# Sums of weight blocks for a seven-product block scheme: from accumulating transfers to VectorE additions in the raw buffers

## What is computed

```python
def swiglu(h, w_in, w_out):
    gate, up = jnp.split(h @ w_in, 2, axis=-1)
    return (jax.nn.silu(gate) * up) @ w_out
```

## Time and profile before

| | |
|---|---|
| median of three runs | 1367.05 us (1366.12 to 1367.58) |
| the profiled execution, its own time | 1369.06 us |
| its span | 1367.1 us |
| mean granted TensorE clock | 0.988 |
| TensorE / VectorE / ScalarE / GpSimd busy | 95% / 63% / 43% / 11% |

### The profile page before, as it was taken

One profiled execution on the slowest core, in us unless ns is written; L12 is line 12 of the kernel. 1 busy time (PEld: TensorE's weight loads), 2 busy tenths in 40 slices (PEclk: granted clock), 3 DMA queues, 4 the chain that ended last, 5 costly groups with the idle time before them and its releaser, 6 DMA issues. The chain is left out here.

```text
span 1367.1 us, 18309 instructions
## 1 busy us (share of the span) xinstructions
PE 1305.5 (95%) x6963; PEld 1072.3 (78%) x6963; DVE 867.1 (63%) x1512; ACT 588.4 (43%) x1113; POOL 147.5 (11%) x160
## 2 busy tenths in 40 slices
PE   3799999999999999999999999999999999999998
PEld 3678788889788888888888876655887888888886
DVE  4889787647567755666565759876463574457235
ACT  3256674545453222321224655687353342333231
POOL 1002020004400000000000001221011001000000
PEclk9899999999999999999999999999999999999999
DMA  9654522110516555555543120010139468736221
GB/s 322 196 172 149 185 66 90 63 62 2 185 43 208 199 188 175 197 201 185 189 138 93 44 74 31 32 32 32 62 101 232 129 153 229 173 90 183 65 92 62
DMA packets 110408, 175.17 MB, mean 128 GB/s; under 512 B 9709, under 2 KB 74490, under 8 KB 110330
## 3 DMA queue, kind: packets, MB, share of 16 engines
q1 hardware_dynamic: 90970, 113.30, 25.2%
q0 software_dynamic: 19360, 60.82, 15.8%
HBM read 172.01 MB, written 2.10 MB: 127 GB/s over the span
## 5 line engine op out<-in xcount | busy, mean ns | idle before, releaser
L411 PE MATMUL ps<-h_hi,w_hi 128*128 128x512 f32 x872 | 343.7, 394 | 1.8 <-DVE w_lo L395 1.4
L413 PE MATMUL ps<-h_hi,w_lo 128*128 128x512 f32 x872 | 340.2, 390 | 0.0
L412 PE MATMUL ps<-h_lo,w_hi 128*128 128x512 f32 x872 | 339.9, 390 | 0.0
L395 DVE TENSOR_TENSOR w_lo<-raw,w_hi 128x1024 fp32r<-128x1024 f32 x156 | 189.5, 1224 | 183.8 <-ACT w_hi L389 183.1
L389 ACT ACTIVATE w_hi<-raw 128x1024 fp32r<-128x1024 f32 x158 | 165.3, 1051 | 97.8 <-PE ps L2444 69.7
L411 PEld LDWEIGHTS ps<-h_hi,w_hi 128*128 128x128 f32 x872 | 164.2, 188 | 35.8 <-ACT silu_g L2266 1.3
L413 PEld LDWEIGHTS ps<-h_hi,w_lo 128*128 128x128 f32 x872 | 164.0, 188 | 35.0
L412 PEld LDWEIGHTS ps<-h_lo,w_hi 128*128 128x128 f32 x872 | 164.3, 188 | 33.0
L514 DVE SCALAR_TENSOR_TENSOR ada_acc<-ada_in,c_act,ada_acc 128x512 f32<-128x512 f32 x154 | 115.6, 751 | 4.2
L2266 ACT ACTIVATE silu_g<-ps 128x512 f32<-128x512 f32 x44 | 26.2, 595 | 127.6 <-PE ps L413 118.2
L1070 DVE SCALAR_TENSOR_TENSOR tmp<-conv_u,conv_t,tmp 128x512 f32<-128x512 f32 x72 | 54.2, 752 | 37.0 <-ACT tmp L1064 34.9
(11 more groups left out here) (429 smaller groups left out, 2485.7 us busy)
## 6 DMA issues: line engine op xcount, KB each, us to landing
raw<-in_ffn_w_in_dram SPq DMA_DIRECT2D x44, 1024.0 KB, 5.4
ada_in<-in_ada_w_dram POOLq DMA_DIRECT2D x40, 1024.0 KB, 5.7
raw<-in_gdn_w_in_dram SPq DMA_DIRECT2D x16, 1024.0 KB, 5.8
ada_in<-in_ffn_w_out_dram POOLq DMA_DIRECT2D x14, 1024.0 KB, 10.9
raw<-in_ffn_w_out_dram SPq DMA_DIRECT2D x12, 1024.0 KB, 5.1
ada_in<-in_ada_w_dram SPq DMA_DIRECT2D x4, 1024.0 KB, 9.4
x_t<-in_x_dram SPq DMA_DIRECT2D x2, 2048.0 KB, 9.9
early_slab<-in_ada_w_dram SPq DMA_DIRECT2D x4, 1024.0 KB, 14.1
```

Source lines behind the costliest of these rows:

```text
L395: ops.tensor_tensor(lo, raw_tile(s, kc) if src is None else src, f32(hi), ALU.subtract).then_inc(lo_done, 1)
L411: nc.tensor.matmul(out_, hi[:, k, :], r_hi[:, k, :], start=k == 0, stop=False)
L412: nc.tensor.matmul(out_, hi[:, k, :], r_lo[:, k, :], start=False, stop=False)
L413: last = nc.tensor.matmul(out_, lo[:, k, :], r_hi[:, k, :], start=False, stop=k == kc - 1)
```

## The change

The accumulating transfers go. GpSimd's queue now loads W10 and W11 as they are into `W_SUM[0]` and `W_SUM[1]`; SP loads W00 and W01 into the raw buffers. VectorE makes the sums in place: `raw[0]` becomes W00+W01, then +W11, then +W10, each when the split of the content before is done, and `raw[1]` becomes W01+W11. The products come in the order in which these sums arise: W00, W00+W01, W00+W01+W11, W11, W01+W11, W10, the sum of all. Two products now follow each other in one bank pair, so 14 evacuations are left of 16. The next part's first load into `raw[0]` waits for the last sum's split (`all_lo`), that into `raw[1]` for the split of W01+W11; SP issues them in this order.

```diff
-                    early = (4 * q - 4, 4 * q - 2) if layer in SEVEN and p and isinstance(i, int) and i == 0 else None
+                    early = seven_free(layer, p - 1) if layer in SEVEN and p and isinstance(i, int) and i == 0 else None
...
-                    sp.dma_start(as_quarter(raw[side])[:, k0:k1, :], quarter(layer, p, side, side)[:, k0:k1, :])\
+                    sp.dma_start(as_quarter(raw[side])[:, k0:k1, :], quarter(layer, p, 0, side)[:, k0:k1, :])\
                         .then_inc(raw_in[side], 16)
-            sp.wait_ge(lo_done, u + 6)
-            sp.dma_start(W_SUM[layer][0][:, :, :], quarter(layer, p, 1, 0)).then_inc(sem("last_in"), 16)
+
+        def seven_free(layer, p):
+
+            q, n, _ = part_quads(layer, p)
+            return (sem("all_lo"), 2 * part_no(layer, p) + 2), (lo_done, 4 * (q + n) + 10)
...
-                begin_pool(pool, layer, p)
-                for k in range(2):
-                    add_three(pool, layer, p, k)
-                    add_four(pool, layer, p, k)
-                add_four(pool, layer, p, 2)
-                for side in range(2):
-                    add_two(pool, layer, p, side)
+                for d in range(2):
+                    pool.dma_start(W_SUM[layer][d][:, :, :], quarter(layer, p, 1, d)).then_inc(sem(f"row_in{d}"), 16)
...
+        def add_three(dve, layer, p, s):
+
+            q, n, _ = part_quads(layer, p)
+            dve.wait_ge(sem("row_in1"), 16 * part_no(layer, p) + 16)
+            dve.wait_ge(lo_done, 4 * (q + n) + 2 + s + 1)
+            nc.vector.tensor_tensor(block_half(raw[0], s), block_half(raw[0], s), block_half(W_SUM[layer][1], s),
+                                    ALU.add).then_inc(sem("three_made"), 1)
...
+            for s in range(2):
+                add_three(dve, layer, p, s)
+                seven_split(dve, layer, p, b, s)
+            seven_y(dve, layer, p, 1, 2, 2, 1, 1, None if new else ALU.subtract)
+            for s in range(2):
+                add_right(dve, layer, p, s)
+                seven_split(dve, layer, p, b, 2 + s)
+            seven_y(dve, layer, p, 2, 4, 4, 0, 1, None if new else ALU.subtract)
+            for s in range(2):
+                seven_split(dve, layer, p, c, s)
+                add_four(dve, layer, p, s)
+            seven_y(dve, layer, p, 3, 6, 2, 0, 1, ALU.subtract)
+            for s in range(2):
+                seven_split(dve, layer, p, c, 2 + s)
+                all_split(dve, layer, p, s)
+            seven_y(dve, layer, p, 4, 8, 4, 1, 1, ALU.subtract)
             dve_split(dve, nxt, 0)
+            seven_y(dve, layer, p, 5, 10, 0, 0, 0, ALU.add)
             dve_split(dve, nxt, 1)
...
             product(4, plain(0, 0), ring(0), True, first_free, split_to(0), made(1))
+            product(2, mixed(0), ring(1), True, ups_read, split_to(2), made(3))
             product(4, mixed(1), ring(0), False, read_to(read), split_to(4), made(3))
+            product(2, mixed(2), ring(1), False, read_to(read + 2), split_to(6), made(4))
             product(4, plain(0, 1), ring(0), False, read_to(read + 4), split_to(8), made(1))
+            product(0, plain(1, 0), ring(1), True, gates_read, split_to(10), made(2))
+            product(4, plain(1, 1), summed, False, read_to(read + 8),
```

More of the change, by code:

```diff
@@ L346, in load_quad @@
                 if free is not None:
-                    sp.wait_ge(lo_done, free[side])
+                    sp.wait_ge(*free[side])
                 elif not (isinstance(q, int) and q == 0):
@@ new lines, in block_half, with add_two @@
+        def block_half(t, s):
+            return flat(t[:, :, :])[:, s * 1024:(s + 1) * 1024]
+        def add_two(dve, layer, p, s):
+            q, n, _ = part_quads(layer, p)
+            dve.wait_ge(raw_in[1], (q + n) * 16 + 48)
+            dve.wait_ge(lo_done, 4 * (q + n) + s + 1)
+            nc.vector.tensor_tensor(block_half(raw[0], s), block_half(raw[0], s), block_half(raw[1], s), ALU.add)\
+                .then_inc(sem("two_made"), 1)
+        def add_three(dve, layer, p, s):
+            q, n, _ = part_quads(layer, p)
+            dve.wait_ge(sem("row_in1"), 16 * part_no(layer, p) + 16)
+            dve.wait_ge(lo_done, 4 * (q + n) + 2 + s + 1)
+            nc.vector.tensor_tensor(block_half(raw[0], s), block_half(raw[0], s), block_half(W_SUM[layer][1], s),
+                                    ALU.add).then_inc(sem("three_made"), 1)
@@ new lines, in add_four, with add_right @@
+        def add_four(dve, layer, p, s):
+            q, n, _ = part_quads(layer, p)
+            dve.wait_ge(sem("row_in0"), 16 * part_no(layer, p) + 16)
+            dve.wait_ge(lo_done, 4 * (q + n) + 4 + s + 1)
+            nc.vector.tensor_tensor(block_half(raw[0], s), block_half(raw[0], s), block_half(W_SUM[layer][0], s),
+                                    ALU.add).then_inc(sem("four_made"), 1)
+        def add_right(dve, layer, p, s):
+            dve.wait_ge(sem("two_made"), 2 * part_no(layer, p) + s + 1)
+            nc.vector.tensor_tensor(block_half(raw[1], s), block_half(raw[1], s), block_half(W_SUM[layer][1], s),
+                                    ALU.add).then_inc(sem("right_made"), 1)
@@ new lines, in seven_src @@
+        def seven_src(layer, p, q, s):
+            at = 2 * (q - part_quads(layer, p)[0] - PARTS[p] // 2) + s // 2
+            made, row = 2 * part_no(layer, p) + s % 2 + 1, 16 * part_no(layer, p) + 16
+            block = (raw[0], raw[0], raw[0], W_SUM[layer][1], raw[1], W_SUM[layer][0])[at]
+            signal = (raw_in[0], sem("two_made"), sem("three_made"), sem("row_in1"), sem("right_made"), sem("row_in0"))[at]
+            return block_half(block, s % 2), signal, (q * 16 + 48, made, made, row, made, row)[at]
@@ L2033, in all_split_act @@
         def all_split_act(act, layer, p, q, s):
[L2035 removed]
+            act.wait_ge(sem("four_made"), 2 * part_no(layer, p) + s + 1)
             act.wait_ge(lo_done, q * 4 + s + 3)
[L2037 removed]
+            nc.scalar.activation(ALL[layer][0][:, s, :], block_half(raw[0], s),
                                  ACT.Copy)\
@@ L2044, in all_split @@
             dve.wait_ge(sem("all_hi"), 2 * part_no(layer, p) + s + 1)
-            nc.vector.tensor_tensor(lo[:, s, :], flat(W_SUM[layer][1][:, :, :])[:, s * 1024:(s + 1) * 1024],
+            nc.vector.tensor_tensor(lo[:, s, :], block_half(raw[0], s),
                                     f32(hi[:, s, :]), ALU.subtract).then_inc(sem("all_lo"), 1)
@@ L2159, in seven_dve @@
-            seven_y(dve, layer, p, 5, 12, 0, 0, 0, ALU.add)
+            seven_y(dve, layer, p, 6, 12, 4, 1, 0, None if new else ALU.add)
             dve_split(dve, nxt, 2)
             dve_split(dve, nxt, 3)
-            ada(1, 3)
-            seven_y(dve, layer, p, 6, 14, 4, 1, 0, None if new else ALU.add)
         def seven_pe(pe, layer, p):
@@ L2168, in seven_pe @@
             done = part_no(layer, p)
-            u, read, f0 = 4 * (q + n), 16 * done, 16 * done
+            u, read, f0 = 4 * (q + n), 14 * done, 16 * done
             all_hi, all_lo = ALL[layer]
```

74 lines of the change are left out of this document (8 added, 66 removed).

## The result

The changed kernel takes 1377.21 us (median of four runs, 1375.99 to 1377.32); the kernel before, beside it, 1366.59 (four runs, 1365.65 to 1367.58). The ratio is 1.0071, interval 1.0058 to 1.0083: slower by 0.7%. The profiled execution after took 1377.32 us, span 1375.6, mean granted clock 0.988.

What follows compares the result with a forecast made beforehand. TensorE, busy throughout both seven-product stages at full clock, was taken as the bound. New waits of 5.9 us (part 0) and 6.3 (part 1), 12.2 together, less 1.9 returned, gave +10.3 on 1367.05: 1377.3 us, range 1372 to 1383.

Steps and rivals of the forecast that it cites:

- product 3, first half: Part 0's stage: an evacuation pair, addition, ScalarE's rounding and split make product 3's first matmul 1.4 us late.
- product 3, second half: Part 0's stage: the second half block goes the same round of addition, rounding and split, 2.2 us late.
- product 4, second half: Part 0's stage: VectorE puts an evacuation pair, two additions and two splits ahead; second split 0.3 us late.
- product 6, second half: Part 0's stage: four-block additions, an evacuation pair and the last sum's round trip delay the second split 0.9 us.
- next quad: Behind part 0's stage: raw buffer 0 is loaded only once the last sum is split; first matmul 1.1 us late.
- the two waits ahead: Ahead of part 0's stage: two TensorE waits blamed on accumulating transfers go, returning 1.9 us; bounds 0 and 1.9.
- The price of an addition: Each of eight in-place 128x1024 additions a part on VectorE takes 1.23 us, like a split.
- Rival (c): Additions on VectorE cost only 0.69 us: +2.7 us, 1369.8 us, no change that could be told; chance 0.06.
- The alternation: In the stages VectorE stands still while ScalarE rounds each sum (1.05 us), once per half block, before splitting it.
- The late load: SP's load into raw buffer 0 for the next quad, issued after the last sum's split, lands after 5.1 us.
- rival (b): The next quad's load lands in 9.8 us, not 5.1; each part loses 4.7 more, 1386.7 us; chance 0.08.
- rival (a): TensorE's clock also falls behind product 3's waits, once per part: 3.4 us more, 1380.7 us; chance 0.10.

Runs made afterwards that it cites:

- The first experiment: Changed kernel with product 3's two additions run back to back, then the two splits: 1373.12 us, ratio 1.0031 to the kernel before.
- the second: Changed kernel with VectorE's whole stage order rewritten, two additions a part moved into the last quad's epilogue: 1364.35 us, ratio 0.9968 to the kernel before.
- the last experiment: Reordered kernel with two plain and five accumulating transfers put back ahead of part 0's two plain loads: 1370.87 us, ratio 1.0016 to the kernel before.

## Why the prediction was right

The working went along VectorE's order, and VectorE's order is where the time was. The mechanism held step by step, not only the sum. How late each matmul came, in part 0 (its distance from the start before it, less the usual 0.227, plus what its successor lost behind a slower first matmul):

| step | forecast | measured |
|---|---|---|
| product 3, first half | 1.4 | 1.43 - 0.23 + 0.08 = 1.28 |
| product 3, second half | 2.2 | 2.21 - 0.23 + 0.11 = 2.09 |
| product 4, second half | 0.3 | 0.39 - 0.23 + 0.11 = 0.27 |
| product 6, second half | 0.9 | 1.01 - 0.23 + 0.11 = 0.89 |
| next quad | 1.1 | 1.29 - 0.23 + 0.08 = 1.14 |
| part 0 | 5.9 | 5.73 by the stage's length |
| part 1 | 6.3 | 6.35 |
| the two waits ahead | -1.9 | -2.03 |
| all | +10.3 | +10.2 |

That the median, 1377.21, lies 0.1 us from the forecast is luck on top of this: small misses of both signs cancel in the sum, the forecast stood on a median of three runs, 1367.05, where four gave 1366.59, and medians of the unchanged kernel wander by more than a microsecond. What the runs bear out is +10.2 beside +10.3 by stage lengths.

- **The price of an addition** was taken from the split's row, 1.23 us; it measured 1.22, in place or not. Rival (c), an addition at 0.69 us, falls. The Trainium skill, "VectorE: DVE Perf Modes", section on the perf-mode tier table, leaves an fp32 tensor_tensor at the single rate; the trace agrees (1.22 us, where the one-source cast of the earlier trace rows takes 0.69).
- **The alternation** was the step that mattered: an addition, 1.13 us of standing still, a split. The first experiment takes one such turn away and 2.4 us with it, and the second all of them and all the loss.
- **VectorE's amount of work** was in the walk too, as the evacuation and the two additions that stand ahead of product 3. Reordering inside the stage leaves 1.4 and 1.7 us a part, which moving two additions out of the stage removes.
- **The late load** was put at 5.1 us to landing. The last sum's split frees the buffer at 1129.44 + 1.23 = 1130.67 and ScalarE starts on the load at 1135.97: 5.3. The price of rival (b), 9.8, was a median of five loads beside accumulating transfers (6.9 to 21.5 us singly). None of these is left, and GpSimd's own two loads are issued at 1138.44, after the late load has landed. The reading that the loads behind the two waits took 9.8 us was wrong (19.3 and 21.5), but the sum does not use it.
- **The return of 1.9 us** was counted as the whole of the two waits ahead of part 0, and the whole came back (2.03 by lengths). The issues between 1010 and 1062 us, after:

```profile
raw<-in_ffn_w_in_dram SPq DMA_DIRECT2D x6, 1024.0 KB, 5.2
ada_in<-in_ffn_w_out_dram POOLq DMA_DIRECT2D x2, 1024.0 KB, 6.7
```

- **The clock**, rival (a), stayed where it was. Windows of 2 us over product 3's two waits, after:

```profile
1106.00:1108.00 2.00, 0.96 (x5) 0.64 (x4) 2.00 (x2) 0.00 (x0) 0.00 (x0) 1.00 0.00 0
1108.00:1110.00 2.00, 0.94 (x5) 0.41 (x3) 0.87 (x2) 1.62 (x2) 0.00 (x0) 1.00 0.01 4
1110.00:1112.00 2.00, 1.25 (x5) 1.05 (x6) 2.00 (x4) 1.33 (x2) 0.00 (x0) 1.00 0.00 0
```

TensorE was busy for half of these 6 us, and the granted clock is 1.00 in all three, the level of 2.4 GHz.

## What to carry to other kernels

When work is moved onto an engine that runs in order, cost its place before its duration: here an instruction whose successor needed another engine's answer to it cost that answer's time as well (1.13 us), on an engine that is busy only 64% of the span. Put something ready between the two (an evacuation, the other half's addition), and write out the starts of engine after engine until the one that sets the end: here this walk gave each wait to 0.13 us, while the busy shares showed nothing. And a change that loses as a whole can hold a part that gains: the plain loads were worth 2 us, and in the right order they were what was left of the change.

## What had not been expected of the hardware

- **An accumulating transfer takes about twice the DMA time of a plain one.** The same 7.34 MB took 67.4% of the 16 DMA engines' time from 1010 to 1062 us in the kernel before (two plain, five accumulating), and 39.5% as seven plain transfers. If a plain one costs a seventh of 39.5%, 5.6%, the five accumulating ones cost (67.4 - 2 x 5.6) / 5 = 11.2% each, twice as much. That split is worked out and not measured by itself, but the changed kernel's two plain ones took 11.3% in the same window, and the packets say nearly the same: 1904 / 7 = 272 for a plain one, (3184 - 2 x 272) / 5 = 528 for an accumulating one. GpSimd, too, is occupied longer by issuing one: 1.27 to 1.33 us beside 0.75. Whether TensorE pays is another matter: in the kernel before, part 1's five accumulations cost it no wait.
- **Where the clock falls isn't told by one wait's length.** In the last experiment it fell behind a wait of 2.30 us, to 0.50 of full speed, the level of 1.2 GHz, in one slice of 2 us. In the kernel before, a wait of 2.37 left it at 1.00, and so did waits of 1.04 and 1.81 with 1.4 us of work between them here. What tells these cases apart stays open; no run was made for it.
- **The row that ends a wait can be the wrong place to mend.** The next quad's wait was put down to an evacuation; moving the evacuation gained 0.7 us a part and an earlier load all 1.1.
